# Delta-rule stage: half of the gate projection between the decay groups, rows scaled beside them, SiLU of z behind the inversion

## What is computed

```python
proj = x @ w_in
qkv, z, b, a = split(proj)
qkv = silu(causal_dwconv(qkv, conv_w))
q, k = l2norm(q) * GDN_DK ** -0.5, l2norm(k)
beta = sigmoid(b)
g = -exp(a_log) * softplus(a + dt_bias)
# per chunk of 64
g = cumsum(g)
decay = exp(where(causal, g[:, None] - g[None, :], -inf))
lmat = where(strict, (k * beta) @ k.T * decay, 0)
t_inv = inverse(eye + lmat)
u, w = t_inv @ (v * beta), t_inv @ (k * beta * exp(g))
a_intra = (q @ k.T) * decay
# a scan over the chunks carries a state of 128 x 128 a head
o = o * rsqrt(mean(o * o) + eps) * norm_g * silu(z)
out = o @ w_out
```

## Time and profile before

| what | value |
|---|---|
| median of 3 runs | 1650.14 us (1649.18 to 1650.91) |
| span of the profiled execution | 1646.0 us |
| mean granted TensorE clock | 0.966 |
| TensorE busy | 1528.1 us (93%), 10172 instructions |
| VectorE busy | 1043.1 us (63%), 1535 instructions |
| ScalarE busy | 665.1 us (40%), 841 instructions |
| GpSimd busy | 19.5 us (1%), 13 instructions |
| HBM read | 440.75 MB, 268 GB/s over the span |

### The profile page before, as it was taken

One profiled execution on the slowest core, in us unless ns is written; L12 is line 12 of the kernel. 1 busy time (PEld: TensorE's weight loads), 2 busy tenths in 40 slices (PEclk: granted clock), 3 DMA queues, 4 the chain that ended last, 5 costly groups with the idle time before them and its releaser, 6 DMA issues.

```text
span 1646.0 us, 23842 instructions
## 1 busy us (share of the span) xinstructions
PE 1528.1 (93%) x10172; PEld 1146.2 (70%) x10172; DVE 1043.1 (63%) x1535; ACT 665.1 (40%) x841; POOL 19.5 (1%) x13
## 2 busy tenths in 40 slices
PE   7997988999996799999999999899999999999986
PEld 7976947888985688888888888798444434443425
DVE  6647656999789969888898888777211221122117
ACT  5553215434431146776777767344211111111114
POOL 0000000000000000000000000200000000000001
PEclk9998999999997799999999999999999999999999
DMA  9341014463361045998989889359999999999991
GB/s 349 131 156 45 3 45 148 169 247 154 122 235 67 1 160 221 362 353 324 354 308 369 341 336 346 148 195 427 380 428 427 427 428 426 427 428 428 426 394 39
DMA packets 37552, 443.43 MB, mean 269 GB/s; under 512 B 5568, under 2 KB 6080, under 8 KB 10176
## 3 DMA queue, kind: packets, MB, share of 16 engines
q1 hardware_dynamic: 36288, 438.35, 66.7%
q10 hardware_dynamic: 1152, 3.46, 0.6%
HBM read 440.75 MB, written 1.05 MB: 268 GB/s over the span
## 4 chain that ended last, share of the span: by engine, by line
PE 66%; DVE 14%; DMA 6%; issue 2%; ACT 2%; SPq 0%; PEldq 0%; DVEq 0%; PEld 0%; ACTq 0%
PE psum L235 64%; DMA sb_spare<-moe_up 2%; DVE sb_ring_r L1202 2%; DMA sb_ring<-ffn_wide 1%; DMA sb_ring<-moe_wide 1%; DVE sb_split L1866 1%; DVE sb_work L2563 1%; DVE sb_work L1584 1%; DVE sb_work L1585 1%; DMA sb_lnp<-ln_rows 1%; PE psum L2359 1%; DMA sb_ring<-ffn_last 1%; PE psum L1921 1%; DMA sb_work<-b_im 0%; ACT sb_split L1860 0%
## 5 line engine op out<-in xcount | busy, mean ns | idle before, releaser
L1866 DVE TENSOR_TENSOR sb_split<-sb_ring,sb_split 128x2048 fp32r<-128x2048 f32 (+1 forms) x144 | 301.4, 2110 | 46.3 <-ACT sb_split L1860 45.5
L235 PE MATMUL psum<-sb_work 64*64 64x64 f32 (+9 forms) x3008 | 296.0, 373 | 37.1 <-DVE sb_work L1569 13.9
L1860 ACT ACTIVATE sb_split<-sb_ring 128x2048 fp32r<-128x2048 f32 (+1 forms) x144 | 253.3, 1774 | 90.2 <-PE psum L235 58.7
L235 PEld LDWEIGHTS psum<-sb_work 128*64 128x64 f32 (+4 forms) x3008 | 161.0, 157 | 159.7 <-issue 129.0
L235 PE MATMUL psum<-sb_split 128*128 128x512 f32 (+1 forms) x912 | 269.0, 384 | 0.7 <-DVE sb_split L2166 0.7
L235 PE MATMUL psum<-sb_split,sb_lnp_r 128*128 128x512 f32 (+1 forms) x768 | 230.4, 374 | 1.4 <-DVE sb_split L2135 1.4
L235 PEld LDWEIGHTS psum<-sb_split 128*128 128x128 f32 x912 | 169.8, 188 | 31.6 <-DVE sb_split L2166 1.7
L235 PEld LDWEIGHTS psum<-sb_split,sb_lnp_r 128*128 128x128 f32 x768 | 142.7, 188 | 21.8 <-DVE sb_split L2135 1.6
L235 PE MATMUL psum<-sb_xT_r,sb_ring_r 128*128 128x256 f32 x512 | 146.2, 285 | 0.0
L235 PE MATMUL psum<-sb_ring,sb_work 128*64 128x512 f32 (+1 forms) x496 | 127.1, 605 | 6.7 <-DVE sb_work L2563 4.7
L2561 DVE TENSOR_TENSOR sb_work<-sb_work,psum 128x512 f32<-128x512 f32 x16 | 11.0, 688 | 166.9 <-ACT sb_work L2473 166.9
(11 more groups left out here) (427 smaller groups left out, 2624.7 us busy)
## 6 DMA issues: line engine op xcount, KB each, us to landing
sb_ring<-moe_wide SPq DMA_DIRECT2D x48, 2048.0 KB, 8.4
sb_work<-moe_up SPq DMA_DIRECT2D x33, 2048.0 KB, 24.4
sb_ring<-w_dense SPq DMA_DIRECT2D x23, 2048.0 KB, 8.5
sb_ring<-moe_last SPq DMA_DIRECT2D x24, 1536.0 KB, 8.3
sb_ring<-moe_up SPq DMA_DIRECT2D x18, 2048.0 KB, 24.7
sb_work<-moe_down SPq DMA_DIRECT2D x17, 2048.0 KB, 22.7
sb_ring<-ffn_wide SPq DMA_DIRECT2D x12, 2048.0 KB, 8.1
sb_ring<-moe_down SPq DMA_DIRECT2D x9, 2048.0 KB, 23.8
```

The source lines that it names most:

```text
L235: return nc.tensor.matmul(o, lhsT, rhs, start=start, stop=stop, **kw)
L1860: act.activation(wh[half_home(e, i)][:, 0:half_size(i)], half_raw(e, i), ACT.Copy).then_inc(sem("m1_high"), 1)
L1866: v.tensor_tensor(wl[home][:, 0:half_size(i)], half_raw(e, i), wh[home][:, 0:half_size(i)].bitcast(F32), ALU.subtract).then_inc(sem("m1_sp ...
```

## The change

- The second half of the gate projection (pieces 24 + 4 to 24 + 7, `z_piece(1, G)`) is no longer one block ahead of the gates. One piece stands at the end of each decay group on TensorE; its low part stands on VectorE inside the group, behind the decay arguments.
- The separate loop over transposes and scaled rows is gone. Each decay group holds its transposes (banks 0 and 1), and ScalarE alone writes all three scaled copies (`rows_scaled`), `kbg` too, beside VectorE's decay work. The decay arguments and beta rows share one bank (2 or 3 by group), the two products another (4 or 5).
- Sigmoid becomes exponential, add 1 and reciprocal, the latter two on VectorE. The high part of piece 24 + 3 stands ahead of the logarithm, its low part behind the inverse norms. 4 gate matmuls of 16 columns replace 8 of 8.
- z is copied to `zs` unchanged: half 0 ahead of the gate exponentials, half 1 inside level 0 of the inversion (`z_kept`). SiLU runs on `zs` behind the last copy of w, and GpSimd's products behind each half of it.
- The input's high and low parts, the three piece buffers and the mask levels lie elsewhere in SBUF; sizes and numbers of buffers are the same.

```diff
-        A_levels = [Am.rearrange("p i c -> p (i c)")[:, IDX * CHUNK * m:IDX * CHUNK * (m + 1)].rearrange("p (i c) -> p i c", i=IDX)
-                    for m in range(2)]
+        A_levels = [t.rearrange("p i c -> p (i c)")[:, IDX * CHUNK:].rearrange("p (i c) -> p i c", i=IDX) for t in (Wm, gB)]
...
+            for i in range(4):
+                z_piece(0, i)
             pe.wait_ge(sem("conv_done"), QKV)
             pe.wait_ge(sem("silu_done"), QKV)
-            pe.wait_ge(sem("z_done"), 4)
 
             pe.wait_ge(sem("gates_vector"), 3)
...
             for G in range(NGRP):
                 h, h0 = G // 2, HD * (G % 2)
...
                 if G < 2:
-                    pe.wait_ge(sem("kd_done"), G + 3)
-                    pe.wait_ge(sem("kbg_done"), G + 3)
-                    pe.wait_ge(sem("vrows_done"), G + 3)
+                    pe.wait_ge(sem("gates_vector"), (5, 8)[G])
                 else:
                     pe.wait_ge(sem("at_done"), G - 1)
...
+                ins.then_inc(sem("decay_ps"), 1)
+                if G == 0:
+                    pe.wait_ge(sem("z_done"), 2)
...
+                if G >= 1:
+                    pe.wait_ge(sem("rows_done"), G)
+                for i in range(HD):
+                    ins = pe.transpose(bank[0][:, i * P:(i + 1) * P], kT[:, h0 + i, h * P:(h + 1) * P], ident)
+                ins.then_inc(sem("krows_ps"), 1)
+                for i in range(HD):
+                    ins = pe.transpose(bank[1][:, i * P:(i + 1) * P], vT[:, h0 + i, h * P:(h + 1) * P], ident)
+                ins.then_inc(sem("vrows_ps"), 1)
+                if G == 0:
+                    pe.wait_ge(sem("gates_vector"), 2)
+                z_piece(1, G)
+            pe.wait_ge(sem("rows_done"), NGRP)
+            pe.wait_ge(sem("at_done"), NGRP)
...
-            act.activation(beta[:, :, :], ba[:, :, 0:HEADS], ACT.Sigmoid).then_inc(sem("gates_act"), 1)
+            act.activation(beta[:, :, :], ba[:, :, 0:HEADS], ACT.Exp, scale=-1.0).then_inc(sem("gates_act"), 1)
             act_link(act, act.activation(sp_a[:, :, :], sp_a[:, :, :], ACT.Exp, scale=-1.0))
             act.activation(a_log, a_log, ACT.Exp).then_inc(sem("gates_act"), 1)
+            gd_high(act, QKV + 3)
             act.activation(sp_a[:, :, :], sp_a[:, :, :], ACT.Ln, bias=1.0).then_inc(sem("gates_act"), 1)
-            gd_high(act, QKV + 3)
             act.wait_ge(sem("gates_vector"), 2)
             act.activation(rn[:, :, :], rn[:, :, :], ACT.Sqrt).then_inc(sem("gates_act"), 1)
...
+            def z_kept(j, h):
+                act.wait_ge(sem("z_ps"), 2 * j + h + 1)
+                act.activation(zs[:, h, 512 * j:512 * j + 512], bank[4 + 2 * j + h][:, :], ACT.Copy).then_inc(sem("z_done"), 1)
+            gd_high(act, QKV + 4)
+            gd_high(act, QKV + 5)
+            for h in range(HALVES):
+                z_kept(0, h)
...
+            decayed(0)
+            for G in range(NGRP):
+                rows_scaled(G)
+                if G == 0:
+                    gd_high(act, QKV + 7)
+                if G + 1 < NGRP:
+                    decayed(G + 1)
             for g in range(6 * NGRP):
...
+                if g in (2, 3):
+                    z_kept(1, g - 2)
...
+            act.wait_ge(sem("z_done"), 4)
+            for h in range(HALVES):
+                act.activation(zs[:, h, :], zs[:, h, :], ACT.Silu).then_inc(sem("z_done"), 1)
...
+            v.wait_ge(sem("gates_act"), 1)
+            dve_link(v, v.tensor_scalar(beta[:, :, :], beta[:, :, :], 1.0, None, ALU.add))
+            dve_link(v, v.reciprocal(beta[:, :, :], beta[:, :, :]))
+            gd_low(v, QKV + 3)
...
+                if G > 0:
+                    gd_low(v, QKV + 4 + G)
+                v.wait_ge(sem("kq_ps"), G + 1)
                 v.wait_ge(sem("decay_done"), G + 1)
...
-            g.wait_ge(sem("z_done"), 4)
             g.wait_ge(sem("small_loaded"), 16 * NLOADS)
             for h in range(HALVES):
+                g.wait_ge(sem("z_done"), 4 + h + 1)
```

More of the change, by code:

```diff
@@ L457, in wt_ps, with bank_own @@
             return psum[:, b:b + 2, 0:HD * CHUNK].rearrange("p c (i t) -> p c i t", i=HD)
-        def bank_own(b):
-            return bank[b][:, 0:HD * CHUNK].rearrange("p (i c) -> p i c", i=HD)
+        def bank_own(b, part=0):
+            return bank[b][:, HD * CHUNK * part:HD * CHUNK * (part + 1)].rearrange("p (i c) -> p i c", i=HD)
         NGRP = IDX // HD
-        gxh, gxl = (gx_r[:, 2 * D * n:2 * D * (n + 1)].rearrange("p (k t) -> p k t", k=DC) for n in range(2))
+        gxh, gxl = (s5_in_high[:, 2 * n:2 * n + 2, :].rearrange("p a d -> p (a d)").rearrange("p (k t) -> p k t", k=DC)
+                    for n in range(2))
         GD_PIECES = QKV + 8
@@ L576, in gdn_tensor @@
+            mm(bank[3][:, 32:48], cum, g_all)
+            mm(bank[3][:, 48:64], blk, g_all)
+            for c, t in enumerate((first64, last64)):
+                ins = mm(bank[3][:, 64 + 16 * c:80 + 16 * c], t, g_all)
             ins.then_inc(sem("gates_ps"), 1)
@@ L655, in gdn_tensor @@
             pe.wait_ge(sem("t_done"), 5 * NGRP)
+            pe.wait_ge(sem("z_done"), 4)
             for G in range(NGRP):
@@ L767, in gdn_scalar, with rows_scaled @@
                            ACT.Exp).then_inc(sem("gates_act"), 1)
-            act.wait_ge(sem("gates_vector"), 6)
-            for G in range(NGRP):
+            gd_high(act, QKV + 6)
+            def rows_scaled(G):
+                h, h0 = G // 2, HD * (G % 2)
                 act.wait_ge(sem("krows_ps"), G + 1)
-                for i in range(HD):
-                    h, e = G // 2, HD * (G % 2) + i
-                    ins = act.activation(kd[:, HD * G + i, :], bank[4 + G % 2][:, i * P:(i + 1) * P], ACT.Copy,
-                                         scale=kd_s[:, h, e:e + 1])
-                ins.then_inc(sem("kd_done"), 1)
+                for dst, by in ((kd, kd_s), (kbg, kbg_s)):
+                    for i in range(HD):
+                        act.activation(dst[:, HD * G + i, :], bank[0][:, i * P:(i + 1) * P], ACT.Copy, scale=by[:, h, h0 + i:h0 + i + 1])
@@ L777, in gdn_scalar @@
                 act.wait_ge(sem("vrows_ps"), G + 1)
                 for i in range(HD):
-                    h, e = G // 2, HD * (G % 2) + i
-                    ins = act.activation(vb[:, HD * G + i, :], bank[6 + G % 2][:, i * P:(i + 1) * P], ACT.Copy,
-                                         scale=beta[:, h, e:e + 1])
-                ins.then_inc(sem("vrows_done"), 1)
-            for G in range(NGRP):
+                    ins = act.activation(vb[:, HD * G + i, :], bank[1][:, i * P:(i + 1) * P], ACT.Copy, scale=beta[:, h, h0 + i:h0 + i + 1])
@@ L857, in gdn_vector @@
              .then_inc(sem("gates_vector"), 1)
-            for s in range(QKV + 4, GD_PIECES):
-                gd_low(v, s)
+            v.wait_ge(sem("gates_vector"), 3)
+            v.tensor_copy(gBo[:, :, :], bc(g_t.rearrange("p a b -> p (a b)"), 2, CHUNK)).then_inc(sem("gates_vector"), 1)
+            v.wait_ge(sem("gates_act"), 4)
+            dve_link(v, v.tensor_tensor(kb_s[:, :, :], rn[:, :, HEADS:], beta[:, :, :], ALU.mult))
+            v.tensor_copy(kbBo[:, :, :], bc(kb_s.rearrange("p a b -> p (a b)"), 2, CHUNK)).then_inc(sem("gates_vector"), 1)
```

127 lines of the change are left out of this document (42 added, 85 removed).

## The result

| what | value |
|---|---|
| the changed kernel | 1632.73 us median of 4 runs (1630.01 to 1636.82) |
| the kernel before, beside it | 1649.66 us median of 4 runs (1644.4 to 1650.91) |
| ratio | 0.9903, 95% interval 0.9884 to 0.9922 |
| forecast | 1628.5 us, which is 0.9869 of the 1650.14 us it started from; range 0.9848 to 0.9899 |

A forecast was written before the change was run, and what follows sets the result against it. The stage was held bound by hand-offs between engines, not one engine. Gains of 18.2 + 2.9 + 0.5 = 21.6 us take the span from 1646.0 to 1624.4 us; plus 4.1 us gives 1628.5 us, range 1625.0 to 1633.5 us.

The forecast's parts named there:

- Step 1: Before projection piece 4: TensorE's 2.94 us idle stall shrinks to about 0.15 us, and piece 4 ends at 105.1 us.
- rival C: ScalarE's table changes each cost a second wait of 1.4 us, TensorE's new stall grows to 4.3 us: 1632.6 us; chance 0.02.
- Step 2: Gates and first decay group: a new 0.2 us stall ahead of the products, piece 5 ends at 112.0 us.
- Step 3: Decay groups 1 to 3: 5.96 us each, 0.25 us of it waiting; inversion starts at 129.9 us, 18.2 us gained.
- Step 4: Entering the inversion loop: level 1 follows 2.1 us after level 0, gaining 2.9 us; full clock less z copies gains 0.5 us.
- the one on SP's loads: Loads waiting for the last projection piece are released about 10 us later, read far behind by the output projection; cost nothing.
- Step 5: Tail: SiLU of z behind the last evacuation and GpSimd's products beside the first state steps, priced at nothing.
- Rival B: GpSimd's products hold VectorE in the state steps, 3.9 us more: 1632.4 us; chance 0.07.
- Rival A: The clock falls to 0.80 inside the merged stretch, 5 us more: 1633.5 us; chance 0.08.
- Rival D: Engines hand on in series in the decay groups, 14.8 us a group: slower, 1664 us; chance 0.02.
- The slower outcome: Whole kernel slower than before; the forecast gave this 0.02, against 0.97 for faster and 0.01 for no difference.
- The 4.1 us I kept between span and median: Whole kernel: the median before, 1650.14 us, lay 4.1 us above the span of 1646.0 us; added to the forecast span 1624.4.

The follow-up runs named there:

- the gates' edit alone: Kernel before with only the sigmoid as exponential, add and reciprocal, and the fourth piece's high part ahead of the logarithm: 1645.53 us, 0.9966.
- the load held: Changed kernel with the first 2 MB feed-forward weight load held until the inversion's last evacuation: 1629.39 us, 0.9875 of the kernel before.
- the load held to a third: Changed kernel with the first feed-forward weight load released after 8 of the inversion's 24 evacuations, one execution: 1632.93 us.

## Why the prediction was right in kind and wrong in size

**Step 1, the stall before piece 4: right.** Piece 4 follows within 0.17 us (0.15 forecast), and the gates' edit alone shows the same. ScalarE, against the earlier trace rows:

```profile
98.30 1.28 ACT L742 ACT_TABLE_LOAD   x1
99.59 0.22 ACT L742 ACTIVATE sb_front<-sb_front 128x16 f32<-128x16 f32 x1
100.06 1.04 ACT L493 ACTIVATE sb_gw_r<-sb_ring 128x1024 fp32r<-128x1024 f32 x1
101.12 1.28 ACT L746 ACT_TABLE_LOAD   x1
```

A load takes 1.28 us and the activation follows it at once, so rival C's second wait is not there.

**Step 2, gates and first group: right.** Products at 107.24 us without the 0.2 us of stall, group 1 at 112.10 us (112.0 forecast).

**Step 3, the groups: right, 0.9 us short.** A group takes 6.23 us where I had 5.96 us. Without a wait it takes 5.84 us (the first group), not 5.71 us, and the piece waits 0.39 us for its low part, not 0.25 us:

```profile
119.55 0.86 DVE L897 SCALAR_TENSOR_TENSOR sb_work<-psum,sb_front 128x64 f32<-128x64 f32 x4 [1.93 <-PE psum L233]
```

VectorE starts the arguments 1.21 us after the decay set began at 118.34 us; the set itself takes 0.97 us, and the hand-off is 0.24 us where I allowed 0.15. The loop starts at 130.80 us, not 129.9 us: 17.3 us gained of 18.2. Moving the low part gets these waits back and 1.0 us of the start.

**Step 4, into the loop: here it failed.** It has two terms. "Level 1 starts 2.1 us later" was 2.51 us: level 0 goes through two banks, so its third set waits for ScalarE's first copy, and level 1's first set for the third one:

```profile
132.78 0.38 ACT L793 ACTIVATE sb_work<-psum 128x256 f32<-128x256 f32 x1 [0.40 <-PE psum L233]
```

This cost 0.4 us. The large miss is "I take the full clock now ... 0.5 us": 224 matmuls took 11.24 us (133.31 to 144.55 us) where I had 7.8 us, 3.4 us more, although the 1.0 us put in for z's two copies was 0.16 us at most. In their place stand the pause of 2.20 us and 1.64 us lost to the half clock behind it; another 0.45 us is in the first 104 matmuls, a little slower than the price I used. The row I took the clock from was a stretch with no load in it; the sentence that went wrong is the one on SP's loads, "released about 10 us later and ... read by the output projection far behind". I asked who reads that data and not what its transfer runs beside. With the load held, the 224 matmuls take 7.37 us, and the norm ends 3.2 us earlier. In the two later profiles of the changed kernel the 224 matmuls took 8.17 and 9.07 us and yet the norm ended at the same time: there the stops came to 1.5 and 2.2 us, and the rest went at half clock further on. That this half clock follows from the load is not shown. The load's own share is thus 1.5 us (stops alone, second profile) to 3.8 us (2.20 + 1.64, first profile).

For the first profile 0.9 + 0.4 + 3.4 = 4.7 us, and 21.6 - 4.7 = 16.9 us, which is the landmark's 16.95.

**Step 5, the tail: right.** GpSimd's products lie beside the first state steps, and VectorE is not held, against 0.69 us in the earlier trace rows:

```profile
176.55 4.67 POOL L1027 TENSOR_TENSOR sb_work<-sb_work,sb_front 128x1024 f32<-128x1024 f32 x2 [176.10 <-ACT sb_work L801]
```
```profile
177.20 0.69 DVE L972 TENSOR_TENSOR sb_work<-sb_work,psum 64x512 f32<-64x512 f32 x1
```

Rival B is dead, and the rule of the Trainium skill (SBUF — State Buffer, Who interferes with whom) is borne out for a wide operation on both sides: 0.69 us with one input in PSUM, 2.58 us instead of 0.42 us with both in SBUF.

**Rival A** names nearly the measured time, 1633.5 us, and is wrong all the same: the merged stretch ran at 1.00. Rival D, a series of hand-offs, would have shown groups of 14.8 us. The slower outcome was 0.02 and nothing spoke for it.

**The sum.** The median missed the forecast by 4.2 us, and the span by 7.5 us (1631.9 against 1624.4): 4.7 us of it in the stage, and 2.85 us behind it, which executions of one code differ by anyway. The 4.1 us I kept between span and median was 1.8 us in the profiled run of after. The other runs too lie some 1.8 us above their spans, so the profiled execution of before, span 1646.0 us, was most likely some 2.3 us faster than the median, and I started the spans from a low one. The range took its low end from stalls and its high end from rival A, and held nothing for transfers that had changed their place. It was the rival's 5 us, for a cause that did not come, that brought the high end within 0.0004 of the measured ratio; that is luck.

## What to carry to other kernels

When work moves earlier, list every load that its end releases, and look at what the transfer now runs beside, not only at who reads it. A TensorE stretch of many small matmuls needs its own instructions from memory, here 16 KB every 4 us or so, and a 2 MB load in flight with them stopped it for 0.7 to 2.9 us. The sign is an "issue" gap in such code that ends some 1.5 us after a late packet of the instruction queue has landed, and one wait on SP took the long stops away. To see 3 us in a kernel of 1630, compare landmarks inside the stage, counted from a landmark ahead of the change, and run the same code twice, and only then the medians.

## What the runs showed of the hardware that I had not expected

- With the load held to a third, no instruction packet moved for 5.7 us of it, and TensorE stood for 2.88 us. It is not always so long: in the changed kernel's second profile the packet got through 3.7 us after the load's first one, with 2.7 us of load left, and TensorE stood for 0.67 us.
- The load delays instruction packets elsewhere too, without harm: held until the end, it runs from 162.4 to 169.1 us, two packets of instructions lie 6.7 us apart there, and no "issue" stop of 0.2 us follows.
- In these profiles the stretches at half clock last 3.4 or 6.8 us, and behind the one near 44 us they fall elsewhere in each execution: in the changed kernel's stage the next is at 139.6 us in one profile and at 174.3 us in the next. The one follows an idle stretch of 2.20 us, and the two other stops of over 2 us (2.01 and 2.88 us) were followed by one too. The other follows only 0.74 us of idle time, and the 14.4 us ahead of it had TensorE busy for 13.62 us; pauses of 0.67 and 0.85 us in the same execution, and of 1.58 us in the third, brought none. What decides is open.
- The start of the inversion moved by 1.35 us between two executions of the same code (128.96 and 130.31 us), and all of it was there ahead of the changed stretch.
